# The first modulation sums of a decoder layer: from one row per weight tile to four columns per weight tile on TensorE

## What is computed

```python
c_act = jax.nn.silu(c)
mod = c_act @ w_ada[l] + b_ada[l]
shift1, scale1, gate1, shift2, scale2, gate2 = jnp.split(mod[:, None, :], 6, axis=-1)
u = x * (1 + scale1) + shift1
(cb, cc, ch, gq, gk, ...) = jnp.split(u @ w_in[l], split_points, axis=-1)
... three branches, merge, W_o, layer norm, feed-forward, layer norm ...
```

## Time and profile before

| | |
|---|---|
| median of three runs | 2599.48 us |
| the profiled execution | 2600.64 us, of which its span is 2598.9 us |
| TensorE busy | 2539.2 us, 98% of the span |
| VectorE, ScalarE busy | 1728.9 us (67%), 1179.3 us (45%) |
| mean granted clock of TensorE | 0.986 of 2.4 GHz |

### The profile page before, as it was taken

One profiled execution on the slowest core, in us unless ns is written; L12 is line 12 of the kernel. 1 busy time (PEld: TensorE's weight loads), 2 busy tenths in 40 slices (PEclk: granted clock), 3 DMA queues, 4 the chain that ended last, 5 costly groups with the idle time before them and its releaser, 6 DMA issues.

```text
span 2598.9 us, 33407 instructions
## 1 busy us (share of the span) xinstructions
PE 2539.2 (98%) x12104; PEld 2071.6 (80%) x12104; DVE 1728.9 (67%) x2330; ACT 1179.3 (45%) x1477; POOL 85.3 (3%) x89
## 2 busy tenths in 40 slices
PE   7889999999999999999999999999999999999998
PEld 3567888788878887788788888888888888888886
DVE  4677767786578758776666777776765555546556
ACT  2146354635463445535444444434554444453442
POOL 0001010101001100100000000000000000000000
PEclk8799999999999999999999999999999999999999
DMA  9865657656665567555788787887656765666664
GB/s 317 307 201 169 180 171 226 182 175 180 196 215 169 158 201 235 172 154 170 230 267 256 254 264 237 266 257 259 189 170 194 227 185 189 193 184 194 189 185 148
DMA packets 300464, 540.05 MB, mean 208 GB/s; under 512 B 39185, under 2 KB 44817, under 8 KB 299281
## 3 DMA queue, kind: packets, MB, share of 16 engines
q1 hardware_dynamic: 271040, 522.29, 64.8%
q10 hardware_dynamic: 29264, 15.68, 2.0%
HBM read 534.68 MB, written 3.21 MB: 207 GB/s over the span
## 4 chain that ended last, share of the span: by engine, by line
PE 47%; DVE 2%; DMA 1%; issue 0%; ACT 0%; DVEq 0%; SPq 0%; ACTq 0%
PE acc L1798 47%; PE bank L1801 1%; DVE w_lo L1148 1%; DMA raw<-in_w_ff 0%; DMA raw<-in_w_o 0%; DVE z_lo L1132 0%; DVE xr L1138 0%; ACT zw_hi L665 0%; DVE zw_lo L1148 0%; DVE xr L1132 0%; DVE x L1138 0%; DVE xr L1666 0%; DVE ff_part L1760 0%; ACT w_hi L665 0%; DVE macc L1138 0%
## 5 line engine op out<-in xcount | busy, mean ns | idle before, releaser
L1148 DVE TENSOR_TENSOR w_lo<-raw,w_hi 128x1024 fp32r<-128x1024 f32 x788 | 967.2, 1227 | 650.9 <-ACT w_hi L665 606.1
L665 ACT ACTIVATE w_hi<-raw 128x1024 fp32r<-128x1024 f32 x780 | 822.4, 1059 | 1093.2 <-PE acc L1798 761.2
L1798 PE MATMUL acc<-w_hi,u_hi 128*128 128x512 f32 x2272 | 908.6, 400 | 22.3 <-DVE w_lo L1148 21.3
L1798 PE MATMUL acc<-w_hi,u_lo 128*128 128x512 f32 x2272 | 890.2, 392 | 0.0
L1798 PE MATMUL acc<-w_lo,u_hi 128*128 128x512 f32 x2272 | 889.9, 392 | 0.0
L1798 PEld LDWEIGHTS acc<-w_hi,u_hi 128*128 128x128 f32 x2272 | 429.4, 189 | 119.9 <-DVE w_lo L1148 25.5
L1798 PEld LDWEIGHTS acc<-w_hi,u_lo 128*128 128x128 f32 x2272 | 429.3, 189 | 91.6
L1798 PEld LDWEIGHTS acc<-w_lo,u_hi 128*128 128x128 f32 x2272 | 430.0, 189 | 85.2 <-issue 1.0
L1798 PE MATMUL acc<-w_hi,z_hi 128*128 128x512 f32 x880 | 344.0, 391 | 0.2 <-DVE w_lo L1148 0.2
L1798 PE MATMUL acc<-w_hi,z_lo 128*128 128x512 f32 x880 | 342.6, 389 | 0.0
L1798 PE MATMUL acc<-w_lo,z_hi 128*128 128x512 f32 x880 | 342.5, 389 | 0.0
(11 more groups left out here) (266 smaller groups left out, 1568.8 us busy)
## 6 DMA issues: line engine op xcount, KB each, us to landing
raw<-in_w_in SPq DMA_DIRECT2D x416, 512.0 KB, 4.5
raw<-in_w_ff SPq DMA_DIRECT2D x256, 512.0 KB, 4.3
raw<-in_w_ada SPq DMA_DIRECT2D x192, 512.0 KB, 4.8
raw<-in_w_branch_a SPq DMA_DIRECT2D x32, 512.0 KB, 4.9
raw<-in_w_branch_b SPq DMA_DIRECT2D x32, 512.0 KB, 4.9
raw<-in_w_branch_c SPq DMA_DIRECT2D x32, 512.0 KB, 5.1
raw<-in_w_o SPq DMA_DIRECT2D x32, 512.0 KB, 4.9
IT<-decay_d ACTq DMA_DIRECT2D x8, 512.0 KB, 7.6
```

The costliest lines, as they stand in the source:

```text
L665: a.activation(weights(n)[0], raw[:, rl % RAWS, :, :], ACT.Copy).then_inc(hi_ready.sem, 1)
L1148: v.tensor_tensor(lo, raw[:, rl % RAWS, :, :] if src is None else src, hi, ALU.subtract).then_inc(lo_ready.sem, 1)
L1798: return t_.matmul(dst, lhsT, rhs, start=start, stop=stop)
```

## The change

TensorE no longer sums a row. For each of its 47 units the four 128 x 128 blocks of the tile become stationary operands, one after the other, and the matching column of c is the moving operand with one column. Each unit writes four columns of its own in PSUM bank 1 (`first_sums`), with nothing added up in PSUM; `first_columns` writes four more columns for `macc`. VectorE adds up the partial columns of each chunk with one reduction, 8 values per sum for chunk 0 and the odd chunks and 5 for the others, and adds b_ada as before. The row buffer, ScalarE's eight copies of it, the products with the row, and the waits on them are gone. Loads, ring, order and `on_pe` stay.

```diff
+def pe_count(n):
+    return pe_units(n, UPJ - 1) - pe_units(n, -1)
...
+        def first_sums(n, j, count):
+            at = KT + (n * (UPJ + 1) + j) * BPC
+            return bank[1][:, at:at + count * BPC]
...
-            def row_copy(n):
-                act.wait_ge(N["raw_summed"].sem, pe_units(n, UPJ - 1))
-                if n >= 2:
-                    act.wait_ge(N["mcol_summed"].sem, n - 1)
-                activate(row_sb[0:1, n % 2, :], acc[1][0:1, n % 2, :], ACT.Copy, "row_in", n + 1)
...
                 k = BPC * group
-                b = bank[1 - group % 2]
-                tt(mod[:, k:k + BPC], b[:, KT:KT + BPC], bada[:, k:k + BPC], ALU.add)
-                stt(mod[:, KT + k:KT + k + BPC], b[:, KT + BPC:KT + 2 * BPC], 1.0, bada[...], ALU.add, ALU.add)
+                for n in (2 * group, 2 * group + 1):
+                    sums = first_sums(n, 0, pe_count(n) + 1).rearrange("p (j b) -> p b j", b=BPC)
+                    o.do(v.tensor_reduce(mcol[:, n % 2, :], sums, mybir.AxisListType.X, ALU.add))
+                o.after()
+                tt(mod[:, k:k + BPC], mcol[:, 0, :], bada[:, k:k + BPC], ALU.add)
+                stt(mod[:, KT + k:KT + k + BPC], mcol[:, 1, :], 1.0, bada[...], ALU.add, ALU.add)
...
             def first_unit(n, m):
-                if n >= 2 and m == 0:
-                    pe.wait_ge(N["row_in"].sem, n - 1)
-                mm(acc[1][0:1, n % 2, :], c_act[:, k:k + 1], tile[:, 1, :], m == 0, m == UPJ - 1).then_inc(N["raw_summed"].sem, 1)
+                col = first_sums(n, pe_units(n, m) - pe_units(n, -1) - 1, 1)
+                for b in range(BPC):
+                    last = mm(col[:, b:b + 1], tile[:, 1, b * P:(b + 1) * P], c_act[:, k:k + 1])
+                last.then_inc(N["raw_summed"].sem, 1)
 
             def first_columns(n):
-                at = KT + n % 2 * BPC
                 pe.wait_ge(N["macc_summed"].sem, n + 1)
-                pe.wait_ge(N["row_in"].sem, n + 1)
-                if n % 2 == 0 and n >= 4:
-                    pe.wait_ge(N["mod_set"].sem, n // 2 - 1)
+                col = first_sums(n, pe_count(n), 1)
                 for b in range(BPC):
-                    col = bank[1 - n // 2 % 2][:, at + b:at + b + 1]
-                    mm(col, macc[:, n % 2, b * P:(b + 1) * P], ones[:, 0:1], True, False)
-                    last = mm(col, row_sb[0:1, n % 2, b * P:(b + 1) * P], ones[0:1, 0:1], False, True)
+                    last = mm(col[:, b:b + 1], macc[:, n % 2, b * P:(b + 1) * P], ones[:, 0:1])
                 last.then_inc(N["mcol_summed"].sem, 1)
...
-                        if n == 3:
-                            pe.wait_ge(N["rows_in"].sem, 1)
                         first_columns(n - 1)
```

More of the change, by code:

```diff
@@ L341, in layer_program @@
         lnc = sb("lnc", [P, 2, KT], at=lnc_at)
-        row_sb = sb("row_sb", [P, 2, NC], at=w_b_at)
         log_s = sb("log_s", [P, MT, NSM], at=w_b_at + 8 * MT * P)
@@ L407, in layer_program @@
                 ident_made=1, masks_made=1, c_turned_in=1, c_made=1, x_turned=1, x_copied=1, rows_turned=1, rows_in=1,
-                macc_summed=1, mcol_summed=1, mod_set=1, raw_summed=1, row_in=1, u_even=1, u_odd=1,
+                macc_summed=1, mcol_summed=1, mod_set=1, raw_summed=1, u_even=1, u_odd=1,
                 u_hi_made=1, u_lo_made=1, small_done=1, small_in=1, small_neg=1, small_exp=1, small_sp=1, logs_made=1,
@@ L699, in _ @@
             act.dma_start(ws[:, :, 2 * VH:NSM], w_in_t[:, :, OFF_F:OFF_F + FH]).then_inc(ws_in.sem, 16)
-            def row_copy(n):
-                act.wait_ge(N["raw_summed"].sem, pe_units(n, UPJ - 1))
-                if n >= 2:
-                    act.wait_ge(N["mcol_summed"].sem, n - 1)
-                activate(row_sb[0:1, n % 2, :], acc[1][0:1, n % 2, :], ACT.Copy, "row_in", n + 1)
-            row_copy(0)
             for n in range(4):
@@ L725, in _ @@
             o.after()
-            row_copy(1)
             for group in range(FIRST_GROUPS):
@@ L739, in _ @@
                     first_hi(u)
-                if group < FIRST_GROUPS - 1:
-                    row_copy(2 * group + 2)
-                    row_copy(2 * group + 3)
             o.end()
@@ L1227, in first_u @@
                 k = BPC * group
-                b = bank[1 - group % 2]
-                tt(mod[:, k:k + BPC], b[:, KT:KT + BPC], bada[:, k:k + BPC], ALU.add)
-                stt(mod[:, KT + k:KT + k + BPC], b[:, KT + BPC:KT + 2 * BPC], 1.0, bada[:, KT + k:KT + k + BPC], ALU.add, ALU.add)
+                for n in (2 * group, 2 * group + 1):
[3 more added lines that the diff above has]
+                tt(mod[:, k:k + BPC], mcol[:, 0, :], bada[:, k:k + BPC], ALU.add)
+                stt(mod[:, KT + k:KT + k + BPC], mcol[:, 1, :], 1.0, bada[:, KT + k:KT + k + BPC], ALU.add, ALU.add)
                 o.after()
```

## The result

The kernel after takes 2612.15 us (median of six runs, 2606.70 to 2616.44), the kernel before 2599.91 in the same comparison: a ratio of 1.0043, with a 95% interval of 1.0031 to 1.0056.

A forecast was written before the change was run, and what follows sets the result against it. TensorE's chain was taken as the bound. Terms of 10.7, 8.4, 8.4 and 5.2 us sum to 32.7, making 2633.3 us for the profiled execution and 2632 us for the median; range 2614 to 2648.

The forecast's parts named there:

- The bound: Rounds between first jobs: TensorE is tightest, busy 27.60 of 30.93 us, so a round's gain or loss enters the time in full.
- The clock: TensorE's new units: one-column products run at 1.2 GHz, save the first 3.3 us after a job.
- Rival 2: All new units: the clock never falls from 2.4 GHz; sum -9.8 us, 2590, faster; chance 0.08.
- rival 4: First jobs: they stay at 1.2 GHz to their end, 3.3 us more each, four times, 13 us: 2645; chance 0.12.
- Rival 1: Chunk 1: the clock stays at 2.4 GHz because transposes stand between units; the 10.7 us fall away, 2621.5; chance 0.18.
- The price of a call: One-column products on TensorE: 0.31 us a call at full clock, 0.51 at 1.2 GHz; a unit 1.24 or 2.04 us.
- it is dearer at either level: New unit on TensorE: 1.24 us at full clock, 2.04 at 1.2 GHz, against 0.88 for the old at full clock.
- Rival 3: Units on TensorE: weight loads run in the shadow of earlier matmuls, a unit 0.86 us; 2584, faster; chance 0.03.
- up to the end of the first job: Chunk 1 and first job: end moves from 60.22 to 70.9 us, +10.7, with -3.1 to +3.0 for the transposes.
- the two full rounds: From the end of a job to the next start: 25.8 us instead of 17.37, +8.4, twice.
- the jobs in between: First jobs between rounds: they start at 1.2 GHz before and after, on the same chain, so 0 change.
- The guess of 0.25 us for a transpose at 1.2 GHz: Chunk 1's 37 transposes on TensorE: 0.25 us each, between 0.165 and 0.33, 9.25 us in all.

The follow-up runs named there:

- fewer: The kernel after, with 32 units on TensorE instead of 47 and VectorE taking 15 tiles more; 2593.25 us, 0.9973.
- mix: Kernel before, `first_columns` without alternating block heights, VectorE adding up, every second TensorE unit of each chunk (20 of 47) in the new form; 2619.58 us, 1.0068.

## Why the prediction was half right

**The bound, right.** TensorE's chain sets the round, and what a round gains or loses goes into the time: three units less gave back 5.2 us a round, and 11.75 us at the start of the last job stand against 12.2 in the time.

**The clock, right in its place, by its rows.** In the kernel after the clock fell 2.4 to 2.7 us behind the end of each of three jobs (in the slices at 66, 101 and 135 us), with nothing but one-column products since, and it stayed at 1.2 GHz for seven units, with TensorE busy throughout; the sum had 3.3 us. The Trainium skill's page "TensorE: Matmul & The Clock Gate" asks, in "Why this matters for your kernels", for an engine that is kept continuously busy. The slice at 72 us, busy for 1.00 at a clock of 0.50, shows that this was not enough here. Rival 2 is out, and rival 4 too, for the clock came back in the middle of each job (0.87 in the slice at 94 us). Rival 1 did not come true: in chunk 1 a unit and four transposes took 2.62 us (24.51 to 27.13), where 2.4 GHz would make them 1.5, by estimate from 0.21 a call and 0.165 a transpose. But it was not far off: in `fewer`, with 21 transposes on end ahead of them (30.98 to 35.12), units of the same form in chunk 1 took 0.81 us (35.12 to 35.93), the speed of 2.4 GHz. What in a product counts for the clock was not settled: bfloat16 fillers between the calls put its fall off and did not prevent it, and with long float32 products between the new units (`mix`) it came back among the units in one round of three.

**The price of a call, wrong: this is the step that failed.** The prediction took 0.31 and 0.51 us from `first_columns`, the very form as it said, and overlooked that there one-row blocks stand between the 128-row ones. Alone a call costs 0.21 and 0.43 us, so a unit 0.86 and 1.71 instead of 1.24 and 2.04. With these two prices and all else as it stands, the prediction's sum comes to about 13.5 us (7.1, 3.0, 3.0 and 0.5) instead of 32.7, where 11.75 were measured: this term is most of the miss. It follows that the sentence "it is dearer at either level" is false: at the same clock the new unit costs about what the old one costs (`mix`), and the loss is the clock's, but for the 0.4 us that the reductions add to a round. Rival 3 had the price at 2.4 GHz right (0.86 a unit), yet not the clock, which took it back. The Trainium skill's page "TensorE: Matmul & The Clock Gate" gives, in its section "LDWEIGHTS (loading the stationary operand)", the number of columns over 1.2 as the time of a load in ns, by estimate 107 ns for 128. The trace agrees at 2.4 GHz (0.21 us for a call of two loads with their matmuls) and not at 1.2 GHz, where a load with its matmul takes 0.215 us.

**Term by term**, from the starts and ends of the jobs: up to the end of the first job +4.3 us (64.55 against 60.22) instead of +10.7, of which 1.2 is the job itself, 12.37 us long and not 13.56; the two full rounds +4.0 (64.55 to 85.87 against 17.36) and +3.8 instead of +8.4 each; the last +1.2 (17.64 against 16.46) instead of +5.2; the jobs in between -0.9 and -0.6 instead of 0, since the clock came back earlier in them, in the second already in the slice at 94 us of a job that began at 85.87. The sum is 11.8. The guess of 0.25 us for a transpose at 1.2 GHz was near: 0.22 (four from 26.24 to 27.13). The reductions made the wait ahead of a job 1.47 us, where 1.38 was forecast and 1.08 stood before.

**The range.** Its low end came from the clock alone (rival 1); a cheaper call at 1.2 GHz was not among its ends, because the price was taken as seen. A bound below it stood in the earlier trace rows, a load of 0.107 us, and was used for a rival and not for the range.

## What to carry to other kernels

A price read from a stretch holds for that order of instructions: before taking it over, look whether its neighbours are the same as in the new place. And when two forms cost the same at the same clock, the clock decides: here one-column products with 128 x 128 stationary blocks, one behind the other, let TensorE fall to half speed while its row says busy, so read the granted clock beside the busy time. Where both kinds of block are needed, put like with like: `first_columns` fell so from 2.48 to 1.96 us, the clock held behind it, and both together were worth 9 us here.

## What else the runs showed

The granted clock is recorded as 1.00 from the start of each execution here until its first change, and that is not always what TensorE ran at: in the kernel after the slice at 57 us counts four 512-column products under PEclk 1.00, as the one at 93 us does under 0.50, and the slices at 96 and 97 us count six under a true 1.00. The speeds of known products, not the column, tell the clock of that first stretch. And 512-column bfloat16 products with a stationary operand of one column, set between one-column float32 ones, took 0.52 us each at 1.2 GHz, and made their neighbours 0.52 instead of 0.43.
